# Residual rows read before the combination, and key tiles computed once instead of twice

## The chip, the cores and the metric

The kernel runs on one core of one Trainium2 chip. The metric is the device time of one execution, in microseconds. Everything is float32.

## What is computed

The reference is two models in a row on 512 tokens of width 1024.

The first has two layers over 528 positions (16 meta tokens in front). Each layer mixes attention with a recurrent branch and then runs a mixture of experts: a router picks one of 4 groups and 2 of its 8 experts for every token, each chosen expert computes `(silu(x w1) * (x w3)) w2`, and the layer ends in

```
y = gate0 * expert_row0 + gate1 * expert_row1          (per token)
h = layer_norm(ALPHA * h + y) * ln2_g + ln2_b
```

The second model is one block with three branches on 512 latent tokens and 256 context tokens. Branches a and b are attentions with 8 query heads and 2 key/value heads of 64: a sees a window, b everything. Keys are `h @ w_in[:, key columns]`, 128 columns for each branch (head 0 in the first 64, head 1 in the last). Those of b are normalised (`rms_norm`), and the latent keys of both are turned by a rotary embedding; context keys are not.

## The kernel before, in words

The program is a list of stages. Within a stage every engine has its own instruction list and they meet through semaphores; at a stage's end all engines meet, SyncE clears the stage's semaphores, and they meet again. So nothing of one stage's compute overlaps the next stage's. DMAs are issued by SyncE (SP queue), ScalarE (ACT queue) and GpSimd (indirect ones).

**The experts' stage** (`experts`) walks over blocks of 64 token slots. For each block SyncE loads the expert's weights w1, w3 (`load_up`) and w2 (`load_down`, line 1944), 1 MB each, into one of two ring buffers as they come free; GpSimd gathers the block's token rows from `h_rows` in DRAM; TensorE transposes them, multiplies by w1 and w3 (line 2002), transposes the hidden rows and multiplies by w2 (line 2021); ScalarE stores the result into `y_rows` in DRAM with two DMAs of 128 KB (line 2078). Four experts' weights were loaded ahead of the stage, into buffers of their own (`k.early`, on the right side of SBUF); the first of them, `k.early[0]`, is used by the stage's first block and not again. SyncE's last instruction in the stage is the last `load_down`, which waits for the block three before the end. ScalarE waits for its last stores to land before it leaves the stage.

**The combination** (`combine`), once per layer, follows. The 528 tokens are 6 tiles of 88 rows. SyncE reads the residual rows of each tile from `h_rows` (line 2155, six DMAs of 352 KB). GpSimd gathers the two expert rows of each token from `y_rows` (line 2161, two indirect DMAs of 352 KB a tile, 12 in all), tile 0 first. ScalarE scales the first row by its gate (`weigh`, line 2185) once both gathers of the tile have landed; VectorE adds the second (line 2222) and the residual (line 2227), which together with the mean (line 2230) is `add_rows`; ScalarE squares and takes the root; VectorE normalises (`norm`, lines 2234 and 2236), TensorE transposes (line 2174), and the two engines empty PSUM into `k.h` (`finish`, lines 2203 and 2242). VectorE's order is add 0, add 1, norm 0, add 2, norm 1, finish 0, add 3, norm 2, finish 1, and so on. `k.right`, which holds the early buffers, is closed before it.

**The projections of attention** (`scale_inputs`, then `attend`). `scale_inputs` norms the inputs of the second model and meanwhile loads the first weights: 2 MB for b's queries and the key columns. `attend` then computes tiles of 128 output columns, 8 contraction steps each, two matmul instructions a step in the records. The tiles in order: 4 of b's queries, 8 of keys, 4 of a's queries, 6 of values. A key tile is (branch, head g, context or latent): the 64 columns of head g stand twice in the loaded weights, so that the tile holds the same head's keys in partitions 0 to 63 and again in 64 to 127. Tiles of b are followed by a matmul that sums squares (line 2467) and a norm on VectorE, latent ones of both branches by a matmul that turns them (line 2477). TensorE runs through all this in a written order; ScalarE copies each tile out of PSUM (line 2486). SyncE reloads the weight ring for a's queries after tile 4 (line 2429) and for the values after the last key tile.

**The attention itself** (`branch_attention`) computes two query heads at a time (`score`, line 2620): head e = 0 from partitions 0 to 63, e = 1 from 64 to 127, both against the keys of the same head g. That is why the keys stand in both halves.

Of the kernel before, what the change touches and what calls it, by code (L numbers as in the profile page):

```python
# [16 lines left out]
P = 128  # L17
D = 1024
KD = D // P
SEQ, META = 512, 16  # L20
T = SEQ + META
TC = 88
NC1 = T // TC
# [33 lines left out]
CTX = 256  # L57
# [1048 lines left out]
def rwkv(k, a, li):  # L1106
    nc, ps = k.nc, k.ps
    r, key, v = (k.u[:, n * RT:(n + 1) * RT, :] for n in range(3))
    decay_in, rate_in, gate_in = (k.u[:, 3 * RT + n, :] for n in range(3))
    with ExitStack() as tmp:  # L1110
        kk = k.sb("kk", [P, RT, T], stack=tmp)
        sig = [k.sb(f"sig{d}", [P, RT, T], stack=tmp) for d in range(2)]
        rate = [k.sb(f"rate{d}", [P, RT, T], stack=tmp) for d in range(2)]
        y = k.sb("y", [P, RT, T], stack=tmp)
        rwkv_prep(k, a, li, key, v, decay_in, rate_in, gate_in, kk, sig, rate, y)
        wkv(k, a, r, key, v, kk, sig, rate, y)
        k.right = ExitStack()
        k.early = [early_place(k, n) for n in range(SOON)]
        k.early_in = [k.right.enter_context(nc.semaphore(f"early_in{n}")) for n in range(PRE)]
        mix_close(k, a, li, r, key, v, rate, sig, kk, y, gate_in)  # L1120
# [521 lines left out]

def expert_weights(a):
    return [a[n].rearrange("l e (p t) n -> (l e) p t n", p=P) for n in ("moe_w1", "moe_w3", "moe_w2")]


def moe(k, a, li):


    nc, ps = k.nc, k.ps  # L1650
    with ExitStack() as tmp:
        def sb(name, shape, dt=F32):
            return k.sb(name, shape, dt, stack=tmp)
        gate = sb("gate", [TC, 2, NC1])
        dest = sb("dest", [TC, 2, NC1], I32)
        slots = sb("slots", [SLOT, NBLK + 1], I32)
        owner = sb("owner", [1, DYN], I32)
        pairs = sb("pairs", [1, 1], I32)
        k.early += [early_place(k, n) for n in range(SOON, PRE)]
        with ExitStack() as rt:  # L1660
            route(k, a, li, rt, gate, dest, slots, owner, pairs)
        with ExitStack() as ex:
            experts(k, a, li, ex, slots, owner, pairs, k.early, k.early_in)
        k.right.close()
        with ExitStack() as cb:
            combine(k, cb, gate, dest)

# [211 lines left out]
def experts(k, a, li, ex, slots, owner, turns_left, early, early_in):  # L1879
# [34 lines left out]
    with k.stage("blank_set", "passed_gp", "passed_pe", "passed_act", *[f"{n}{z}" for n in names for z in Z],  # L1914
# [11 lines left out]
        def _(sp):  # L1926
# [32 lines left out]
            load_down(1, owner[0:1, bass.ds(n_turns * 2 + (AHEAD - 1), 1)], (z, c))  # L1959

# [170 lines left out]
def combine(k, cb, gate, dest):  # L2131
# [3 lines left out]
    hr = k.sb("c_h_rows", [TC, NC1, D], stack=cb)  # L2135
# [4 lines left out]
    with k.stage(*landed_names, *[f"h{j}_in" for j in range(NC1)], "first_weighted", "weighted", "summed", "meant",  # L2140
                 "squared", "rooted", "inverted", "normed", "c_turned", "act_kept", "dve_kept") as (block, *sems):
        landed, h_in = sems[0:NC1], sems[NC1:2 * NC1]
        (first, weighted, summed, meant, squared, rooted, inverted, normed, turned, act_kept,
         dve_kept) = sems[2 * NC1:]
# [6 lines left out]

        @block.sync
        def _(sp):
            for j in range(NC1):
                sp.dma_start(hr[:, j, :], k.h_rows[j * TC:(j + 1) * TC, :]).then_inc(h_in[j], 16)
# [62 lines left out]
        def _(dve):  # L2218
            def add_rows(j):
# [5 lines left out]
                dve.wait_ge(h_in[j], 16)  # L2225
                pt = row(j).rearrange("s (p t) -> s p t", t=KD)
                dve.scalar_tensor_tensor(pt, hr[:, j, :].rearrange("s (t p) -> s p t", t=KD), ALPHA, pt,
# [10 lines left out]
            def finish(j):  # L2238
# [5 lines left out]
                last.then_inc(dve_kept, 1)  # L2244
            add_rows(0)
# [39 lines left out]
def scale_inputs(k, a, t, x, mod, gain, hl, hc, w_in, ring, ring_in):  # L2285
# [8 lines left out]
    with k.stage("ctx_landed", "squared", "squared_ctx", "summed", "summed_ctx", "root", "root_ctx",  # L2294
# [5 lines left out]
        def _(sp):  # L2300
# [80 lines left out]
def attend(k, a, at, w_in, hl, hc, ys, cq, lf, cv, ring, ring_in):  # L2381
# [11 lines left out]
    tiles = ([("q", 1, m, 1) for m in range(4)] + [("k", n, g, c) for n in (1, 0) for g in range(2) for c in range(2)]  # L2393
# [7 lines left out]
    def home(i):  # L2401
        kind, n, m, lat = tiles[i]
        if kind == "q":
            return q[n][:, m, :]
        return v[:, m, :] if kind == "v" else (kt[n][:, m, CTX:W] if lat else kt[n][:, m, 0:CTX])
# [10 lines left out]
    with ExitStack() as t:  # L2416
# [5 lines left out]
        with k.stage("table_in", "qa_in", "v_in", "made", "emptied", "summed", "rooted", "normed", "turned", "roped",  # L2422
                     "ab_chain", also=ring_in) as (
                block, table_in, qa_in, v_in, made, emptied, summed, rooted, normed, turned, roped, steps):
# [10 lines left out]
            def _(pe):  # L2435
                for what, i in order:
                    kind, n, m, lat = tiles[i]
                    w = cols(i)
                    if what == "tile":
# [4 lines left out]
                        if i == 4:  # L2444
                            pe.wait_ge(k_in, 16 * 8)
# [6 lines left out]
                        for f in range(KD):  # L2452
                            if kind == "q":
                                l, r = ring[0][:, f, m * P:(m + 1) * P], hl[:, f, :]
                            elif kind == "k":
                                l, r = ring[1][:, f, (2 * n + m) * P:(2 * n + m + 1) * P], (hc, hl)[lat][:, f, :]
# [24 lines left out]
            def _(act):  # L2481
                for what, i in order:
                    w = cols(i)
                    if what == "tile":
# [7 lines left out]
                        last.then_inc(emptied, 1)  # L2492
                    elif what == "sum":
# [31 lines left out]
def branch_attention(k, a, at, w_in, hl, hc, q, kt, v, ys, cq, lf, cv):  # L2525
# [61 lines left out]
    with k.stage("tables_in", "wc_even", "wc_odd", "scored", "peaked", "weighed", "sunk", "normed", "turned",  # L2587
# [24 lines left out]
        def _(pe):  # L2612
            def score(i):
# [3 lines left out]
                for bank, off, cols, key in pieces(tiles):  # L2617
                    for e in range(2):
# [3 lines left out]
                                         rhs=kt[n][hd, g, key:key + cols], start=True, stop=True)  # L2622
# [1121 lines left out]
```

## Time and profile before

| | us |
|---|---|
| median of 3 runs | 3941.36 (3934.95 to 3941.69) |
| the profiled execution, its own time | 3947.0 |
| its span in the profile | 3945.2 |
| TensorE busy | 3355.2 |
| VectorE busy | 1496.2 |
| ScalarE busy | 811.6 |

Times in rows are microseconds from the start of the span. A timeline row gives the start, the time that the group of instructions covers, the engine, the line, what is written and read, how many instructions are merged, and in brackets how long the engine had been idle before and what ended that. An engine's name with a q behind it (SPq, ACTq) is the queue side of the engine: the instruction that issues a DMA, not the transfer. A window row gives, for each engine, the busy time, then the clock granted to TensorE (1.00 is full), the mean busy share of the 16 DMA engines and what they moved.

### The profile page before, as it was taken

Reading aid. Unit: us, or ns where it says so; the run is one execution under the profiler, and the core shown is the slowest. Engines: PE = TensorE matmul, PEld = TensorE weight load, DVE = VectorE, ACT = ScalarE, POOL = GpSimd, SP = SyncE. Lnnn points to the kernel's source line nnn. Section 1 sums busy time; section 2 is a strip of 40 time slices with the busy share of each in tenths; the row PEclk is TensorE's granted clock in tenths of the full one; section 3 lists DMA queues with packets and bytes.
Section 4 is the critical chain, followed back from the end, with each engine's and each line's share of the span. In section 5 each row is a group of like instructions: output and inputs, shape, how many; then the busy total and the mean of one; then the engine's idle time right before and its main releaser. Section 6 shows DMA issues by size and latency. Waiting matters only on the chain. (4 is left out here: it accounts for less than half of the span.)

```text
span 3945.2 us, 73875 instructions
## 1 busy us (share of the span) xinstructions
PE 3355.2 (85%) x31960; PEld 2250.6 (57%) x31960; DVE 1496.2 (38%) x2771; ACT 811.6 (21%) x1670; POOL 308.1 (8%) x499
## 2 busy tenths in 40 slices
PE   4898799986874897889958747999988899999998
PEld 0666599774443665789745423567656644444443
DVE  2244455532113444455441125355456521144411
ACT  3111322111112112222021123133343100010000
POOL 0000112001111000211001110000033000000000
PEclk7999799988996998899969977999999999999999
DMA  8210300227994010300148983110010122222221
GB/s 295 74 48 25 129 4 4 77 97 283 395 368 128 32 33 25 131 4 5 76 166 351 411 280 80 33 33 22 12 54 1 66 74 70 80 75 75 62 71 39
DMA packets 181484, 422.88 MB, mean 107 GB/s; under 512 B 33897, under 2 KB 128489, under 8 KB 152633
## 3 DMA queue, kind: packets, MB, share of 16 engines
q1 hardware_dynamic: 162201, 384.26, 26.5%
q0 software_dynamic: 8736, 17.32, 1.7%
q10 hardware_dynamic: 10240, 16.79, 1.3%
q8 instruction: 244, 4.00, 0.4%
q14 instruction: 63, 0.52, 0.0%
HBM read 401.60 MB, written 50.54 MB: 115 GB/s over the span
## 5 line engine op out<-in xcount | busy, mean ns | idle before, releaser
L3401 PE MATMUL ps<-h_lat,wt 128*128 128x512 f32 x704 | 304.7, 596 | 5.9 <-ACT h_lat L3458 5.9
L2002 PE MATMUL ps<-e_w,e_xt 128*64 128x256 f32 x1792 | 226.6, 409 | 64.0 <-DMA e_w<-in_moe_w 62.5
L709 PE MATMUL ps<-h,win 128*128 128x264 f32 x960 | 233.1, 397 | 16.9 <-DVE pad L858 15.3
L2002 PEld LDWEIGHTS ps<-e_w,e_xt 128*64 128x64 f32 x1792 | 149.9, 148 | 162.9 <-issue 78.9
L3401 PEld LDWEIGHTS ps<-h_lat,wt 128*128 128x128 f32 x704 | 134.6, 191 | 176.0 <-issue 174.4
L709 PEld LDWEIGHTS ps<-h,win 128*128 128x128 f32 x960 | 180.7, 193 | 67.4 <-issue 38.7
L2109 DVE TENSOR_TENSOR e_hid<-ps,e_silu 64x256 f32<-64x256 f32 x64 | 39.3, 614 | 399.5 <-ACT e_silu L2068 399.5
L3358 PE MATMUL ps<-h_lat,wt 128*128 128x512 f32 x384 | 169.5, 600 | 9.9 <-DMA wt<-in_w_in 9.9
L3419 PE MATMUL ps<-ff_up,wt 128*128 128x512 f32 x352 | 152.2, 592 | 0.0
L1315 PE MATMUL ps<-inv,nt 48*48 48x48 f32 x3520 | 130.5, 207 | 12.0 <-issue 10.8
L1414 DVE COPY_PREDICATED inv<-level,ps 112x384 f32<-112x384 int32 x176 | 103.5, 588 | 84.1 <-PE ps L1315 75.5
L3358 PEld LDWEIGHTS ps<-h_lat,wt 128*128 128x128 f32 x384 | 73.8, 193 | 103.1 <-issue 93.0
L2021 PE MATMUL ps<-e_w,e_hid_t 128*64 128x512 f32 x448 | 112.8, 622 | 18.5 <-DMA e_w<-in_moe_w 13.9
L1248 ACT ACTIVATE nt<-ps 112x192 f32<-112x192 f32 x220 | 72.6, 330 | 231.2 <-PE ps L1304 228.0
L1315 PEld LDWEIGHTS ps<-inv,nt 48*48 48x48 f32 x3520 | 109.4, 123 | 14.8 <-issue 13.4
L1304 PE MATMUL ps<-inv,by_bet 48*48 48x48 f32 x3520 | 104.9, 206 | 11.9 <-issue 5.9
L3419 PEld LDWEIGHTS ps<-ff_up,wt 128*128 128x128 f32 x352 | 66.9, 190 | 84.2 <-issue 83.7
L1312 PE MATMUL ps<-nt,inv 48*48 48x48 f32 x2816 | 104.2, 207 | 4.7 <-issue 3.7
L2174 PE MATMUL ps<-ident,c_y 88*128 88x88 f32 x96 | 17.2, 361 | 101.1 <-DVE c_y L2236 101.1
L1304 PEld LDWEIGHTS ps<-inv,by_bet 48*48 48x48 f32 x3520 | 93.7, 122 | 16.1 <-issue 9.6
L2072 ACT ACTIVATE e_hid_t<-ps 128x128 f32<-128x128 f32 x64 | 17.7, 277 | 401.5 <-PE ps L2010 401.5
L2663 PE MATMUL ps<-wc,h_lat 128*128 128x256 f32 x384 | 91.5, 383 | 5.8 <-DVE log_f L2774 4.7
(564 smaller groups left out, 6386.6 us busy)
## 6 DMA issues: line engine op xcount, KB each, us to landing
e_w<-in_moe_w SPq DMA_DIRECT2D x168, 1024.0 KB
wmod<-in_w_mod SPq DMA_DIRECT2D x24, 1024.0 KB, 14.2
early<-in_moe_w SPq DMA_DIRECT2D x24, 1024.0 KB, 14.8
wt<-in_w_up SPq DMA_DIRECT2D x22, 1024.0 KB, 5.1
y_rows<-e_y ACTq DMA_DIRECT2D x128, 128.0 KB
win<-in_w_in SPq DMA_DIRECT2D x10, 1536.0 KB, 6.6
wt<-in_w_in SPq DMA_DIRECT2D x12, 1024.0 KB, 7.7
wt<-in_w_down SPq DMA_DIRECT2D x16, 704.0 KB, 4.8
```

What stands on the lines that cost most here:

```text
L709: last = pe.matmul(ps[:, 7, 0:HT], lhsT=ring[(s + 1) % 2][:, i, o:o + P], rhs=k.h[:, i, h * HT:(h + 1) * HT], start=(i == 0), stop=(i == K ...
L1248: act.activation(nt[z][:, :, :], ps[0:R, bank_a(c), 0:RT * WC].rearrange("p (f n) -> p f n", f=RT), ACT.Copy).then_inc(x_kept[z], 1)
L1304: last = pe.matmul(ps[hw, a0, f * WC:(f + 1) * WC], lhsT=by_bet[z][hw, f, 0, :], rhs=inv[z][hw, 0, f, :], start=True, stop=True)
L1312: pe.matmul(ps[hw, a0, f * WC:(f + 1) * WC], lhsT=inv[z][hw, 1, f, :], rhs=nt[z][hw, f, :], start=True, stop=True)
L1315: last = pe.matmul(ps[hw, a0, (RT + f) * WC:(RT + f + 1) * WC], lhsT=nt[z][hw, f, :], rhs=inv[z][hw, 1, f, :], start=True, stop=True)
L1414: dve.copy_predicated(inv[z][0:R, :, :, :], k.level[0:R, level, d:d + 2, None, :].to_broadcast([R, 2, RT, WC]), ps[0:R, a0, 0:2 * RT * WC] ...
L2002: last = pe.matmul(ps[half, 2 + z, 0:EH], lhsT=xt[z][:, f, :], rhs=w[:, f, :], start=(f == 0), stop=(f == KD - 1))
L2021: last = pe.matmul(ps[half, 4 + z, :], lhsT=hid_t[z][:, t, :], rhs=m2[:, t, q * 512:(q + 1) * 512], start=(t == 0), stop=(t == 1))
L2663: last = pe.matmul(ps[:, 7, 0:cols], lhsT=lhsT, rhs=rhs, start=(i == 0), stop=(i == KD - 1))
L3358: last = pe.matmul(o, lhsT=w[:, i, m % 2 * P:(m % 2 + 1) * P], rhs=hl[:, i, :], start=(i == 0), stop=(i == KD - 1))
L3401: last = pe.matmul(o, lhsT=w[:, i, m % 2 * P:(m % 2 + 1) * P], rhs=hl[:, i, :], start=(i == 0), stop=(i == KD - 1))
L3419: last = pe.matmul(o, lhsT=w[:, i, :], rhs=up[:, f, :], start=(f == 0), stop=(f == FT - 1))
```

## The change

Residual rows. After its last `load_down`, still in the experts' stage, SyncE issues three DMAs that read all 528 residual rows into the three tensors of `k.early[0]`, two tiles of 88 rows each; it first waits for the block that used those buffers. The combination no longer issues the six DMAs of line 2155; VectorE waits once, for all three reads, before its first `add_rows`. `k.right` is closed after the combination.

Keys. The key columns are loaded once (two DMAs of 512 KB in place of eight of 256 KB). A key tile is (branch, context or latent), 4 in place of 8, with head 0 in partitions 0 to 63 and head 1 in 64 to 127. During the value tiles ScalarE copies each half to the other half's partitions, into a second tile (8 copies of 64 partitions), and `score` takes the tile in which head g stands in the half e.

```diff
+def residual_rows(k):
+    return [t[0:TC, :, :].rearrange("s a b -> s (a b)").rearrange("s (j n) -> s j n", j=2) for t in k.early[0]]
...
         with ExitStack() as ex:
             experts(k, a, li, ex, slots, owner, pairs, k.early, k.early_in)
-        k.right.close()
         with ExitStack() as cb:
             combine(k, cb, gate, dest)
+        k.right.close()
...
             load_down(1, owner[0:1, bass.ds(n_turns * 2 + (AHEAD - 1), 1)], (z, c))
+            z, c = spot(first.index(("early", 0)))
+            sp.wait_ge(down[z], c + 1)
+            for n, dst in enumerate(residual_rows(k)):
+                sp.dma_start(dst, k.h_rows[2 * n * TC:(2 * n + 2) * TC, :].rearrange("(j s) n -> s j n", j=2)
+                             ).then_inc(k.h_back, 16)
...
-        @block.sync
-        def _(sp):
-            for j in range(NC1):
-                sp.dma_start(hr[:, j, :], k.h_rows[j * TC:(j + 1) * TC, :]).then_inc(h_in[j], 16)
...
-                dve.wait_ge(h_in[j], 16)
...
+            dve.wait_ge(k.h_back, 48)
             add_rows(0)
...
-                for g in range(2):
-                    for c in range(2):
-                        at = (4 * n + 2 * g + c) * 64
-                        sp.dma_start(ring[1][:, :, at:at + 64], w_in[:, :, c0 + g * 64:c0 + (g + 1) * 64]
-                                     ).then_inc(ring_in[2], 16)
+                sp.dma_start(ring[1][:, :, n * P:(n + 1) * P], w_in[:, :, c0:c0 + P]).then_inc(ring_in[2], 16)
...
-    tiles = ([("q", 1, m, 1) for m in range(4)] + [("k", n, g, c) for n in (1, 0) for g in range(2) for c in range(2)]
+    tiles = ([("q", 1, m, 1) for m in range(4)] + [("k", n, 0, c) for n in (1, 0) for c in range(2)]
...
+                def swap(i):
+                    n, lat = tiles[i][1], tiles[i][3]
+                    if lat:
+                        act.wait_ge(roped, turned_tiles.index(i) + 1)
+                    elif i in normed_tiles:
+                        act.wait_ge(normed, normed_tiles.index(i) + 1)
+                    else:
+                        act.wait_ge(emptied, i + 1)
+                    for g in range(2):
+                        act.activation(kt[n][(1 - g) * HD:(2 - g) * HD, 1, keys_of(i)],
+                                       kt[n][g * HD:(g + 1) * HD, 0, keys_of(i)], ACT.Copy).then_inc(swapped, 1)
...
                         last.then_inc(emptied, 1)
+                        if V < i <= V + 4:
+                            swap(i - V + 3)
...
-                                         rhs=kt[n][hd, g, key:key + cols], start=True, stop=True)
+                                         rhs=kt[n][hd, (e + g) % 2, key:key + cols], start=True, stop=True)
```

## Rows read from the trace of the kernel before

**Rows 1.** the page: busy time of the engines (us, share of span, instructions)
```profile
PE 3355.2 (85%) x31960; PEld 2250.6 (57%) x31960; DVE 1496.2 (38%) x2771; ACT 811.6 (21%) x1670; POOL 308.1 (8%) x499
```
**Rows 2.** timeline, layer 1, experts' end into the combination (start, us, engine, line)
```profile
1168.21 3.67 PE L2002 MATMUL ps<-e_w,e_xt 128*64 128x256 f32 x32
...
1168.28 0.33 SPq L1944 DMA_DIRECT2D e_w<-in_moe_w  x1
...
1175.56 3.79 ACTq L2078 DMA_DIRECT2D y_rows<-e_y  x4
...
1184.08 2.50 SPq L2155 DMA_DIRECT2D c_h_rows<-h_rows  x6
1184.91 0.98 POOL L2161 DMA_INDIRECT c_y<-y_rows,dest  x1 [27.21 <-POOLq L151]
1186.20 0.98 POOL L2161 DMA_INDIRECT c_y<-y_rows,dest  x1 [0.31 <-issue]
...
1201.20 1.15 ACT L2185 ACTIVATE c_y<-c_y,gate 88x1024 f32<-88x1024 f32 x1 [26.07 <-DMA c_y<-y_rows,dest]
1202.38 1.28 DVE L2222 SCALAR_TENSOR_TENSOR c_y<-c_y,gate 88x1024 f32<-88x1024 f32 x1 [24.34 <-ACT c_y L2185]
...
1205.63 0.15 DVE L2230 TENSOR_SCALAR c_st<-c_st 88x1 f32<-88x1 f32 x1
...
1215.92 1.19 DVE L2242 TENSOR_SCALAR h<-ps,par 128x88 f32<-128x88 f32 x4
...
1217.02 1.27 DVE L2222 SCALAR_TENSOR_TENSOR c_y<-c_y,gate 88x1024 f32<-88x1024 f32 x1
...
1222.36 1.27 DVE L2222 SCALAR_TENSOR_TENSOR c_y<-c_y,gate 88x1024 f32<-88x1024 f32 x1
```
**Rows 3.** timeline, layer 2, the same places
```profile
2332.04 0.98 POOL L2161 DMA_INDIRECT c_y<-y_rows,dest  x1 [26.59 <-POOLq L151]
...
2348.87 1.15 ACT L2185 ACTIVATE c_y<-c_y,gate 88x1024 f32<-88x1024 f32 x1 [26.56 <-DMA c_y<-y_rows,dest]
2350.05 1.28 DVE L2222 SCALAR_TENSOR_TENSOR c_y<-c_y,gate 88x1024 f32<-88x1024 f32 x1 [24.84 <-ACT c_y L2185]
...
2365.83 1.28 DVE L2222 SCALAR_TENSOR_TENSOR c_y<-c_y,gate 88x1024 f32<-88x1024 f32 x1
```
**Rows 4.** busy time by window (engines, PEclk, DMA share, GB/s), experts' end
```profile
1172.00:1175.00 3.00, 2.74 (x20) 1.17 (x18) 0.93 (x2) 1.39 (x4) 0.00 (x0) 1.00 0.53 164
...
1178.00:1181.00 3.00, 0.00 (x0) 0.00 (x0) 0.04 (x1) 0.00 (x0) 0.00 (x0) 0.90 0.38 88
```
**Rows 5.** DMA queues, 1184 to 1188 us (packets, MB, share of 16 engines)
```profile
q1 hardware_dynamic: 185, 0.70, 51.3%
...
q0 software_dynamic: 45, 0.00, 0.5%
```
**Rows 6.** DMA queues, 1203 to 1209 us: the gathers alone
```profile
q0 software_dynamic: 530, 1.30, 101.8%
```
**Rows 7.** the combination's tile c_y: time from issue to landing
```profile
DMA to landing us min/median/max: 11.0/18.4/22.0
```
**Rows 8.** timeline of TensorE in the projection stage of attention
```profile
2476.63 0.59 PE L2467 MATMUL ps<-ab_sq,ones_h 128*128 128x256 f32 x2
2477.06 1.02 PE L2477 MATMUL ps<-k_b,rot 128*128 128x512 f32 x2
...
2494.27 13.90 PE L2460 MATMUL ps<-h_lat,wab 128*128 128x512 f32 x32
```
**Rows 9.** DMA issues, 2440 to 2500 us: line 2429's load, KB, us to landing
```profile
wab<-in_w_in SPq DMA_DIRECT2D x1, 2048.0 KB, 8.1
```
**Rows 10.** timeline, value tiles of that stage
```profile
2546.91 0.38 ACT L2486 ACTIVATE v_ab<-ps 128x256 f32<-128x256 f32 x1 [3.07 <-PE ps L2460]
```
**Rows 11.** the tile e_silu: a copy to other partitions
```profile
L2068 ACT ACTIVATE e_silu<-ps x64: 375/375/377, 931.1 to 2320.4; 64x256 f32<-64x256 f32 x64
```
**Rows 12.** window of the score matmuls alone (line 2620)
```profile
2555.00:2890.00 335.00, 47.79 (x368) 28.85 (x368) 0.97 0.13 42
```

More of the change, by code:

```diff
@@ L1118, in rwkv @@
         k.early = [early_place(k, n) for n in range(SOON)]
+        k.h_back = k.right.enter_context(nc.semaphore("h_back"))
         k.early_in = [k.right.enter_context(nc.semaphore(f"early_in{n}")) for n in range(PRE)]
@@ L2134, in combine @@
     y = k.sb("c_y", [TC, NC1, 2, D], stack=cb)
-    hr = k.sb("c_h_rows", [TC, NC1, D], stack=cb)
+    hr = residual_rows(k)
     sq = k.sb("c_sq", [TC, 2, D], stack=cb)
@@ L2139, in combine @@
     landed_names = [f"y{j}_in" for j in range(NC1)]
[L2140 to L2144, printed above, removed]
+    with k.stage(*landed_names, "first_weighted", "weighted", "summed", "meant", "squared", "rooted", "inverted",
+                 "normed", "c_turned", "act_kept", "dve_kept", also=[k.h_back]) as (block, *sems):
+        landed = sems[0:NC1]
+        first, weighted, summed, meant, squared, rooted, inverted, normed, turned, act_kept, dve_kept = sems[NC1:]
         def row(j):
@@ L2224, in add_rows @@
                 dve.wait_ge(weighted, j + 1)
-                dve.wait_ge(h_in[j], 16)
                 pt = row(j).rearrange("s (p t) -> s p t", t=KD)
-                dve.scalar_tensor_tensor(pt, hr[:, j, :].rearrange("s (t p) -> s p t", t=KD), ALPHA, pt,
+                dve.scalar_tensor_tensor(pt, hr[j // 2][:, j % 2, :].rearrange("s (t p) -> s p t", t=KD), ALPHA, pt,
                                          ALU.mult, ALU.add, accum_out=stat(0, j)).then_inc(summed, 1)
@@ L2404, in home, with keys_of @@
             return q[n][:, m, :]
-        return v[:, m, :] if kind == "v" else (kt[n][:, m, CTX:W] if lat else kt[n][:, m, 0:CTX])
+        return v[:, m, :] if kind == "v" else kt[n][:, 0, keys_of(i)]
+    def keys_of(i):
+        return slice(CTX, W) if tiles[i][3] else slice(0, CTX)
     normed_tiles = [i for i, x in enumerate(tiles) if x[0] != "v" and x[1] == 1]
@@ L2422, in attend @@
         with k.stage("table_in", "qa_in", "v_in", "made", "emptied", "summed", "rooted", "normed", "turned", "roped",
-                     "ab_chain", also=ring_in) as (
-                block, table_in, qa_in, v_in, made, emptied, summed, rooted, normed, turned, roped, steps):
+                     "swapped", "ab_chain", also=ring_in) as (
+                block, table_in, qa_in, v_in, made, emptied, summed, rooted, normed, turned, roped, swapped, steps):
             @block.sync
@@ L2444, in _ @@
                         if i == 4:
-                            pe.wait_ge(k_in, 16 * 8)
+                            pe.wait_ge(k_in, 16 * 2)
                         if i == QA:
@@ L2455, in _ @@
                             elif kind == "k":
-                                l, r = ring[1][:, f, (2 * n + m) * P:(2 * n + m + 1) * P], (hc, hl)[lat][:, f, :]
+                                l, r = ring[1][:, f, n * P:(n + 1) * P], (hc, hl)[lat][:, f, :]
                             else:
```

## The prediction

> **What bounds the kernel now.** I read the page first: TensorE is busy for 85% of the span, no other engine for more than 38% [rows 1]. That is an average. Since the engines meet at each stage's end, a change is worth what it takes off its own stage, so I went to the timeline of the stages that the diff touches.
>
> In the projection stage TensorE is the bound. Its matmul records follow each other without a gap: 32 of 512 columns in 13.90 us [rows 8], while ScalarE sat idle for 3.07 us before a copy of 0.38 us [rows 10].
>
> In the combination TensorE does nearly nothing. The six reads of residual rows are issued at 1184.08, the first gather at 1184.91, and ScalarE, which starts the work of tile 0, stands idle until 1201.20, released by a gather's DMA [rows 2]. Until 1188 us the DMA engines moved 0.70 MB of residual rows and next to nothing of the gathers [rows 5]: the reads were there first and hold the engines. Later, with the gathers alone, those engines are full as well (share 101.8%) and move 1.30 MB in 6 us, 217 GB/s [rows 6]. So the first 16 us of a combination are DMA time, a third of whose load is residual rows: 6 x 352 KB = 2.16 MB beside 4.33 MB of gathers. Behind it, VectorE is the bound: its add of one tile starts 5.34 us after the one before (1217.02, 1222.36) with no idle time noted [rows 2].
>
> **Part 1, the combination's start.** Without the residual reads, tile 0 needs its two gathers only. The second is issued at 1187.18, 2.27 us after the first issue began (1186.20 + 0.98 - 1184.91) [rows 2]. The bytes of a gather begin more than 2.1 us after its issue: the first one's ended at 1185.89, and by 1188 its queue had moved 0.00 MB [rows 5]; I take 2.4. The 0.72 MB of two gathers at 217 GB/s are 3.3 us [rows 6]. Sum: 2.3 + 2.4 + 3.3 = 8.0 us from the first issue to the landing of tile 0. Today it is 1201.20 - 1184.91 = 16.3 us in layer 1 [rows 2] and 2348.87 - 2332.04 = 16.8 us in layer 2 [rows 3]. Gain: 8.3 + 8.8 = 17.1 us. The ends: without the 2.4 us of delay tile 0 lands at 5.6, a gain of 21.9 for both layers; the slowest I allow is a landing as fast as the quickest gather beside the residual reads, 11.0 us [rows 7], for the second one too, so 12.3, and a gain of 8.5.
>
> The Trainium skill (DMA: Bandwidth & Descriptors, section Anatomy of one DMA) gives a DMA issued by GpSimd about 2.0 us plus its bytes at 436 GB/s. By that page, as an estimate, tile 0 would land at 2.3 + 2.0 + 0.8 = 5.1 us and the gain be 22.9. The trace agrees with its fixed part (over 2.1 us) and not with its rate: half of it is what rows show of these gathers.
>
> **Part 2, the pace behind tile 0.** Today VectorE waits for gathers between tiles 0 and 3: add 3 starts 14.64 us after add 0 in layer 1 (1202.38 to 1217.02) [rows 2] and 15.78 us after it in layer 2 (2350.05 to 2365.83) [rows 3]. Between them lie three adds, two norms and one finish. Two steady steps are two of each, 10.7 us; one more add is 3.40 us (1202.38 to 1205.78) and the finish that is not in it 1.19 us [rows 2]: 10.7 + 3.4 - 1.2 = 12.9. A tile's two gathers take 3.3 us of DMA against 5.34 of VectorE, so the gathers stay ahead once tile 0 is there. I allow 0.3 a layer for ScalarE, whose root of tile 0 comes later in the row than in steady state, and take 13.2: gain 1.4 + 2.6 = 4.0 us. Ends: 0 (the gathers keep today's spacing) and 4.6.
>
> **Part 3, where the residual reads go.** SyncE's last weight load is issued at 1168.28 [rows 2]. The three reads follow it in the same queue, all weights ahead of them, so TensorE waits for none of it; the wait on the first block's `down` was fulfilled long ago, and behind SyncE's reads nothing of its own is queued. The DMA engines are 0.53 busy from 1172 to 1175 and 0.38 from 1178 to 1181 [rows 4], with stores. Today 0.70 MB of them had come by 1188 [rows 5]; if their bytes began a microsecond after the issue at 1184.08 (an estimate), that is 0.70 MB in 2.9 us, about 245 GB/s, and at that rate 2.16 MB are 8.8 us of otherwise free engines. From 1172 that is 1181 alone and about 1184 beside the stores. So they land about when the combination begins (1184.08), and tile 0's add, not before 1193, does not wait. What they cost is the last stores: four are issued from 1175.56 to 1179.35 [rows 2], and ScalarE waits for them before the stage ends. Bounds a layer: nothing if the stores slip between, and 6 us if the stores came behind all the reads that are left at 1178 (8.8 less the free half of the time since 1172). In a fair alternation the last pair, 0.38 of 3 us or 1.1 us of engine time [rows 4], takes about double: I take 1.5, so -3.0 us for both layers.
>
> The same page (section Queues, rings and completion order) says that each DMA engine turns between its queues packet by packet; by it the fair share is the right case, and the price would be the 1.1 to 1.5 us used; no run here shows it yet.
>
> **Part 4, the key tiles.** TensorE loses four tiles: two latent (16 records of 512 columns: 13.73 / 2 = 6.87 us, since the 13.90 of [rows 8] hold 0.17 of tail) and two context ones (16 records of 256; two take 2477.06 - 2476.63 = 0.43 us, so 3.44) [rows 8]: 20.6 us. With them go two sums of squares, 0.86 and 0.43, and two turns of 0.86 (two records of 512). Sum 20.6 + 1.3 + 1.7 = 23.6 us. All of it is on the path, as TensorE has no gap there. What could be late next: the weights of a's queries, 8.1 us after their issue [rows 9]. They are issued as the key tiles begin and needed after them; the key tiles still last 20.6 + 4.7 = 25 us (49 today). The value weights are issued when the keys are done and have four query tiles, over 27 us, of cover. The loads of the key columns shrink from 2 MB to 1 MB, in a stage where nothing waits for them: nothing.
>
> The 8 copies are ScalarE's. A copy of 64 partitions by 256 columns into other partitions takes 0.375 us [rows 11]; for 512 columns I take 0.6. Behind a value tile stand at most two of 0.6, with the tile's own 0.38: 1.6 us where 3.07 + 0.38 are free [rows 10]. Two value tiles follow the third pair and one the last. Cost 0, hidden by the value tiles' matmuls; without that cover 8 copies would be 4 us. Bounds for the part: 22 to 25 us.
>
> **Sum.** 17.1 + 4.0 - 3.0 + 23.6 = 41.7 us off 3947.0, the profiled execution's time, gives 3905.3. The median of the runs shown is 5.6 below that execution, so the forecast is 3900. All ends together: gain 21.9 + 4.6 + 0 + 25 = 51.5, or 8.5 + 0 - 12 + 22 = 18.5; times 3890 and 3923.
>
> **Rivals.** (a) The combination gives nearly nothing: the gathers are the DMA load that matters (4.33 of 6.5 MB) and the moved reads hold back the stage before. For it: gathers alone fill the engines [rows 6]. Against: tile 0 waits for two of twelve gathers only. Price: 8.5 - 8, nearly 0, and part 4 alone: 3941.4 - 23.6 = 3918. Chance 0.16.
>
> (b) The key part gives nothing, because ScalarE or VectorE becomes the bound of the key tiles, or a's query weights are late. For it: VectorE norms and turns each tile. Against: the idle times named above. Price: only 18 of 41.7 us: 3923. Chance 0.05.
>
> (c) Slower. The score matmuls go in pairs, one on each half of the partitions, and both halves read the same columns today; after the change they read two different tiles. Were the pairs side by side only for that reason, each would cost double: 47.8 us of matmuls and up to 28.9 of weight loads more [rows 12], 3900 + 77 = 3977 at most. It decides from 50 us, at which the gain is eaten and 0.2% lost. Against it: line 2002 writes two halves from two different moving tensors, w1 and w3, and does 32 records of 256 columns in 3.67 us, 0.115 each [rows 2], where records of 256 columns cost 0.215 each on the whole array [rows 8]. So different moving data do not stop pairs there. Chance 0.03.
>
> (d) The early reads or the copies do not do what they say (VectorE waits for the reads as long as before): within 2 us of (a). In its chance.
>
> **How the numbers follow.** Forecast 0.76, around 3900, own range 3891 to 3910. The rest: (a) 0.16, (b) 0.05, (c) 0.03. The range of 8 in 10 takes in the forecast's ends and most of (a): 3889 to 3917. This kernel's measurement tells no change from one of under 0.2% (8 us). Faster by more: the forecast, (a) and nearly all of (b), 0.95; same 0.02; slower 0.03.
>
> **What would show it.** In the profile after: the first ScalarE instruction of the combination about 8 us after the first gather's issue, not 16; add 3 about 13 us after add 0; the gap from the last store's issue to the first gather (today 1179.35 to 1184.91, 5.6 us) 1 to 2 us longer; SyncE's three issues right behind its last weight load; 4 key tiles, 23.6 us less of the projection stage, no idle TensorE in it, and the score matmuls' busy time at 47.8. A first tile that lands later than 11 us, or an experts' stage longer by 3 us or more, would make the forecast wrong by (a); a longer score window by (c).

## The result and the profile after

| | us |
|---|---|
| before, median of 4 runs | 3941.53 (3934.95 to 3945.72) |
| after, median of 4 runs | 3905.34 (3904.77 to 3905.90) |
| ratio | 0.9899, 95% interval 0.9885 to 0.9913 |
| span in the profile, before and after | 3945.2, 3903.1 |

By the medians the change makes the kernel 36 us faster (0.9%), by the ratio with its interval 40 us (34 to 45). The forecast was 3900, its range 3889 to 3917.

The timeline of the changed kernel, layer 1, from the experts' end into the combination (start, us, engine, line); it answers to [rows 2]:

```profile
1164.08 1.29 SPq L1969 DMA_DIRECT2D early<-h_rows  x3
...
1165.21 3.67 PE L2013 MATMUL ps<-e_w,e_xt 128*64 128x256 f32 x32 [1.70 <-DMA e_w<-in_moe_w]
...
1172.38 1.94 PE L2032 MATMUL ps<-e_w,e_hid_t 128*64 128x512 f32 x8 [0.57 <-DMA e_w<-in_moe_w]
...
1172.56 6.66 ACTq L2089 DMA_DIRECT2D y_rows<-e_y  x4
...
1177.21 0.69 DVE L2129 COPY e_y<-ps 128x512 f32<-128x512 f32 x1 [4.84 <-DMA y_rows<-e_y]
1185.68 0.98 POOL L2166 DMA_INDIRECT c_y<-y_rows,dest  x1 [29.60 <-SPq L149]
...
1194.24 1.15 ACT L2190 ACTIVATE c_y<-c_y,gate 88x1024 f32<-88x1024 f32 x1 [22.11 <-DMA c_y<-y_rows,dest]
...
1195.49 1.28 DVE L2227 SCALAR_TENSOR_TENSOR c_y<-c_y,gate 88x1024 f32<-88x1024 f32 x1 [17.59 <-ACT c_y L2190]
...
1209.51 1.27 DVE L2227 SCALAR_TENSOR_TENSOR c_y<-c_y,gate 88x1024 f32<-88x1024 f32 x1
```

Tile 0 starts 8.56 us after the first gather's issue (1194.24 - 1185.68), where it was 16.29. But the first gather is issued 20.47 us after TensorE's last expert block began (1165.21), where it was 16.70 [rows 2]. VectorE stood idle for 4.84 us before its last copy and was released by a store. In the kernel before it was 1.97 us, and the matmul released it:

```profile
1175.28 1.94 PE L2021 MATMUL ps<-e_w,e_hid_t 128*64 128x512 f32 x8 [0.46 <-ACT e_hid_t L2072]
...
1177.35 0.69 DVE L2118 COPY e_y<-ps 128x512 f32<-128x512 f32 x1 [1.97 <-PE ps L2021]
```

The same places in layer 2, to be read beside [rows 3]:

```profile
2306.20 3.67 PE L2013 MATMUL ps<-e_w,e_xt 128*64 128x256 f32 x32 [1.74 <-DMA e_w<-in_moe_w]
...
2319.01 0.69 DVE L2129 COPY e_y<-ps 128x512 f32<-128x512 f32 x1 [5.65 <-DMA y_rows<-e_y]
2327.69 0.98 POOL L2166 DMA_INDIRECT c_y<-y_rows,dest  x1 [31.59 <-SPq L149]
...
2335.18 1.15 ACT L2190 ACTIVATE c_y<-c_y,gate 88x1024 f32<-88x1024 f32 x1 [22.06 <-DMA c_y<-y_rows,dest]
...
2336.44 1.28 DVE L2227 SCALAR_TENSOR_TENSOR c_y<-c_y,gate 88x1024 f32<-88x1024 f32 x1 [16.74 <-ACT c_y L2190]
...
2349.82 1.27 DVE L2227 SCALAR_TENSOR_TENSOR c_y<-c_y,gate 88x1024 f32<-88x1024 f32 x1
```

Here tile 0 comes 7.49 us after the gather (16.83 before), and the gather 21.49 us after the last block; in the kernel before that was 2315.39 to 2332.04, 16.65 us.

TensorE in the projection stage, then ScalarE in it, which answer to [rows 8] and [rows 10], and third the window row of the score matmuls alone (line 2637; PE busy, PEld busy, clock, DMA share, GB/s), which answers to [rows 12]:

```profile
2436.10 3.62 PE L2464 MATMUL ps<-h_ctx,wab 128*128 128x256 f32 x16
...
2461.63 7.03 PE L2464 MATMUL ps<-h_lat,wab 128*128 128x512 f32 x16
...
2516.05 1.13 PE L2637 MATMUL ps<-k_a,q_a 64*128 64x256 f32 x8 [1.77 <-PEq L151]
```

```profile
2500.91 0.86 ACT L2495 ACTIVATE k_b<-k_b 64x256 f32<-64x256 f32 x2
2503.95 0.38 ACT L2501 ACTIVATE v_ab<-ps 128x256 f32<-128x256 f32 x1 [2.19 <-PE ps L2464]
2504.36 1.28 ACT L2495 ACTIVATE k_b<-k_b 64x512 f32<-64x512 f32 x2
2507.40 0.38 ACT L2501 ACTIVATE v_ab<-ps 128x256 f32<-128x256 f32 x1 [1.76 <-PE ps L2464]
```

```profile
2500.00:2890.00 390.00, 47.79 (x368) 28.84 (x368) 0.98 0.11 36
```

The key tiles begin at 2436.10, a's first query tile at 2461.63: 25.5 us, where 49 were spent. The two copies of a pair take 0.86 us (256 columns) and 1.28 us (512), and ScalarE still sits idle for 1.76 to 2.19 us before the copy of the value tile behind each pair. TensorE's records of the stage show no idle time. From the stage's first matmul to the first score matmul it is 2401.50 to 2516.05, 114.6 us; before, 2417.43 to 2555.49, 138.1. The score matmuls' busy time is 47.79 us, to the hundredth what it was [rows 12].

### The profile page after: what moved, and what is told of

It reads as the page before. It is cut to its first block and busy times, and to the rows that moved or that the text cites. A ratio compares the mean times of both kernels' runs of the same rounds, so it can differ in the third digit from the quotient of the medians.

```text
span 3903.1 us, 73678 instructions
## 1 busy us (share of the span) xinstructions
PE 3331.0 (85%) x31888; PEld 2236.9 (57%) x31888; DVE 1485.6 (38%) x2761; ACT 812.1 (21%) x1670; POOL 314.4 (8%) x499
## 5 line engine op out<-in xcount | busy, mean ns | idle before, releaser
L709 PE MATMUL ps<-h,win 128*128 128x264 f32 x960 | 233.4, 397 | 16.8 <-DVE pad L858 15.2
L1316 PE MATMUL ps<-inv,nt 48*48 48x48 f32 x3520 | 130.9, 207 | 10.6 <-issue 9.2
L1313 PEld LDWEIGHTS ps<-nt,inv 48*48 48x48 f32 x2816 | 88.4, 123 | 9.8 <-issue 8.1
```

The costliest lines, as they stand in the source:

```text
L709: last = pe.matmul(ps[:, 7, 0:HT], lhsT=ring[(s + 1) % 2][:, i, o:o + P], rhs=k.h[:, i, h * HT:(h + 1) * HT], start=(i == 0), stop=(i == K ...
L1313: pe.matmul(ps[hw, a0, f * WC:(f + 1) * WC], lhsT=inv[z][hw, 1, f, :], rhs=nt[z][hw, f, :], start=True, stop=True)
L1316: last = pe.matmul(ps[hw, a0, (RT + f) * WC:(RT + f + 1) * WC], lhsT=nt[z][hw, f, :], rhs=inv[z][hw, 1, f, :], start=True, stop=True)
```

## The experiments

All times are beside runs of the kernel before on the same chip. To read the traces I use one distance that drifts of other stages do not enter, the "whole distance": from TensorE's last w2 block of the experts (1175.28 before, layer 1) to VectorE's last gated add in the combination (add 5, 1227.71). "End" is the part from that block to the first gather, "landing" from there to ScalarE's first instruction on tile 0. The expectations count from the w1 block before it instead, which in the kernel before begins 7.1 us earlier. Each kernel has one trace, so differences under about a microsecond (the changed kernel's two traces differ by 0.6 and 0.7) say little.

| kernel | median | ratio (95%) | end, layers 1, 2 | landing | whole distance |
|---|---|---|---|---|---|
| before | | | 9.6, 9.6 | 16.3, 16.8 | 52.4, 54.1 |
| after | 3905.3 | 0.9899 (0.9885 to 0.9913) | 13.3, 14.0 | 8.6, 7.5 | 47.8, 46.8 |
| after, again | 3911.8 | 0.9922 (0.9906 to 0.9938) | 14.2, 15.1 | 8.4, 7.1 | 48.4, 47.5 |
| keys_only | 3923.3 | 0.9942 (0.9923 to 0.9960) | 9.6, 9.6 | 17.8, 16.8 | 55.2, 53.3 |
| reads_only | 3934.0 | 0.9965 (0.9953 to 0.9977) | 14.7, 15.6 | 8.2, 7.4 | 48.0, 48.2 |
| no_reads | 3897.3 | 0.9873 (0.9851 to 0.9895) | 9.6, 9.6 | 8.7, 7.8 | 43.4, 42.5 |
| late_kept | 3908.6 | 0.9892 (0.9872 to 0.9913) | 15.9, 15.3 | 8.9, 8.1 | 49.8, 48.6 |
| late_out | 3928.5 | 0.9941 (0.9926 to 0.9956) | 11.0, 11.0 | 18.8, 16.9 | 54.9, 53.1 |
| spread | 3923.6 | 0.9922 (0.9907 to 0.9938) | 15.4, 15.5 | 8.5, 7.0 | 49.4, 48.4 |
| late_out_spread | 3924.3 | 0.9926 (0.9910 to 0.9942) | 12.0, 12.1 | 13.4, 13.6 | 51.6, 50.7 |
| early_reads | 3929.5 | 0.9945 (0.9929 to 0.9961) | 9.5, 9.5 | 8.5, 6.8 | 43.4, 42.2 |
| own_buffer | 3906.2 | 0.9914 (0.9901 to 0.9928) | 16.0, 15.0 | 7.6, 7.3 | 48.7, 47.5 |
| gated | 3905.2 | 0.9912 (0.9894 to 0.9929) | 10.6, 10.9 | 7.9, 7.1 | 48.2, 48.5 |
| gated_own_buffer | 3906.1 | 0.9909 (0.9895 to 0.9922) | 9.5, 9.5 | 8.1, 8.4 | 47.8, 47.6 |

Three sets were timed on three chips: keys_only, reads_only, no_reads and late_kept (the kernel before 3945.4), then late_out, spread, late_out_spread and early_reads (3954.5), then the changed kernel again with own_buffer, gated and gated_own_buffer (3941.0). So ratios are compared, not medians, and a time named in an expectation of the first two sets has to be read 4 and 13 us higher. The ratios are estimates of their own; the quotients of the medians differ from them by up to 0.0015. The changed kernel gave 0.9899 and 0.9922, which is how far two sets of runs of one kernel lie apart here.

**Each part alone.** keys_only is the kernel before with the edits of `scale_inputs`, `attend` and `score`; reads_only has the others.

> The key part alone; the residual rows are read as before. Theory (the parts add, and the key part is TensorE's matmuls and nothing else): 23.5 us off the kernel before, 3918, with the combination as it was (tile 0 starts 16 us after the first gather's issue). Rival (part of what the changed kernel gained came from the fewer small DMAs of the key columns or from ScalarE): a gain clear of 23.5, under 20 or over 28.

> The residual rows' part alone; keys as before. Theory (combinations shorter by 8.4 and 11.7 us, experts' ends longer by 3.8 and 4.8): 11 to 13 us off, 3929 to 3931. Rival (the forecast's price of 3 us for the moved reads was right and the profile's longer ends are chance): 18 us off, 3923.

0.9942 is 23 us (16 to 30), 0.9965 is 14 us (9 to 18). The two sum to 37 us; the change as a whole gives 36 by its medians, 40 and 31 by its two ratios. The intervals do not tell 23.5 from 20 by themselves; the traces do: from the projection stage's first matmul to the first score matmul it is 114.3 us in keys_only and 138.1 in reads_only. For the reads, 18 lies at the interval's edge, so the time alone does not decide. The trace of reads_only has the longer ends again (14.7 and 15.6), and its whole distances are 10.3 us shorter in all than those of the kernel before, which speaks for 11 to 13.

**What the moved reads cost.** no_reads leaves out the three reads and the wait for them.

```diff
-            for n, dst in enumerate(residual_rows(k)):
-                sp.dma_start(dst, k.h_rows[...]).then_inc(k.h_back, 16)
...
-            dve.wait_ge(k.h_back, 48)
```

> The changed kernel with the residual reads left out altogether, and VectorE's wait for them (the residual added is then whatever lies in the buffer, so the output is not the reference's). Theory (the moved reads cost 8.6 us through the stores that share the DMA engines): 3896 to 3898, the distance from TensorE's last block of experts to the first gather back at 16.7 us in both layers, and VectorE's last copy there not waiting for a store. Rival (the ends are longer for another reason, such as the later close of the buffers or the barrier): no less than 3903, distance still over 20 us.

0.9873 against 0.9899 is 10 us, and against the second set's 0.9922 it is 19; the traces below give 8.7. The end is back at 9.6 us in both layers, and the copy waits for the matmul only:

```profile
1173.07 1.94 PE L2027 MATMUL ps<-e_w,e_hid_t 128*64 128x512 f32 x8 [0.46 <-ACT e_hid_t L2078]
1173.36 3.79 ACTq L2084 DMA_DIRECT2D y_rows<-e_y  x4
...
1175.14 0.69 DVE L2124 COPY e_y<-ps 128x512 f32<-128x512 f32 x1 [1.97 <-PE ps L2027]
1182.70 0.98 POOL L2161 DMA_INDIRECT c_y<-y_rows,dest  x1 [27.21 <-SPq L149]
```

So the reads cost 4.3 to 4.4 us a layer of the whole distance (47.8 - 43.4, 46.8 - 42.5), 8.7 in all. Left where they were before the change they cost 9.0 and 11.6 a layer (52.4 - 43.4, 54.1 - 42.5). So 11.9 of 20.6 us are gone, a little over half of their price. In the changed kernel their packets last from about 1169 to 1181 us. The DMA queues in those twelve microseconds (packets, MB, share of 16 engines; q1 carries the reads, q10 the stores):

```profile
q1 hardware_dynamic: 544, 2.10, 51.2%
q10 hardware_dynamic: 472, 0.77, 22.6%
```

The reads' 2.10 MB take the whole of it, with all but the last 0.01 MB of the stores among them. Without the reads the stores' last packets had moved by 1181 in the kernel before, and the first gather was issued at 1184.91.

**Reads later.** late_kept and late_out hold the reads back:

```diff
             sp.wait_ge(down[z], c + 1)
+            z, c = in_loop(n_turns, -1)
+            sp.wait_ge(y_kept[z], c + 1)            # late_kept
+            sp.wait_ge(y_out[z], c * 32 + 32)       # late_out, in its place
```

> The changed kernel, but SyncE holds the three residual reads until VectorE has copied the last block's rows out (wait on the last y_kept), so that they run under the last store, the stages' meeting and the first gathers' start-up. Theory: the wait of VectorE's last copy for a store goes (2.8 and 3.2 us), of the last store's own delay about 1 us a layer stays; the reads, 8.8 us, end some 9 to 10 us after that copy, before tile 0's add needs them (17 us after it): 3898 to 3900. Rival A (the reads then run into the gathers and what is won is given back there): 3904 to 3908, tile 0 later than 10 us after the first gather's issue. Rival B (the longer end has nothing to do with the order): 3905.

The copy no longer waited for a store, and yet the end grew to 15.9 us and the ratio is that of the changed kernel: the theory missed, and rival A missed as well (tile 0 came 8.9 us after the first gather, not later than 10). The time is as rival B has it, but the order does matter: it took away the copy's wait and the stores waited elsewhere. The DMA queues of late_kept (packets, MB, share of 16 engines), 1182 to 1185 us and then 1185 to 1188:

```profile
q1 hardware_dynamic: 117, 0.47, 72.6%
q10 hardware_dynamic: 3, 0.01, 1.0%
```

```profile
q1 hardware_dynamic: 120, 0.45, 52.1%
q10 hardware_dynamic: 107, 0.17, 18.6%
```

ScalarE had issued its last store by 1180.40 and SyncE its reads from 1179.12. For three microseconds the stores' queue moved 3 packets, then 107. By 1185 the reads had moved 0.23 MB (1179 to 1182) and 0.47, together 0.70, about one read of the three (0.72). So the last stores stood behind roughly the first read and alternated with the rest, which lasted until about 1195. That it was just this read is my reading of the sums. From 1182 to 1184.5 the stores' queue moved no packet at all, while the reads held 0.73 of the engines' time and a quarter of it was free.

> The changed kernel, but SyncE issues the three residual reads only when the experts' last store has landed. Where the wait stood on y_kept, the last store's packets moved some 6 us late, behind the reads, and the meeting of the engines came 4 us after them while the reads still ran. Theory (stores issued after reads wait behind them, and the stage's end waits for the stores only): the distance from TensorE's last block to the first gather is 16.7 us as without reads; the reads run from about 1181 to 1192, under the meeting and the first two gathers; tile 0 starts 8 to 11 us after the first gather; 3898 to 3901. Rival (the stage's end waits for SyncE's own reads to land): that distance is 16.7 + 9 to 11 us, 26 or more, and the time 3912 or more.

The theory held for the end, but for 1.4 us, and failed for the sum. The end is 11.0 us with the reads in flight, so the stage's end does not wait for SyncE's reads; the 1.4 us over 9.6 I put down to SyncE, which now issues last before the engines meet; no run shows that apart. But tile 0 landed 18.8 us after the first gather. The queues from 1187 to 1192 us show why, with the gathers' issue begun at 1187.16:

```profile
q1 hardware_dynamic: 198, 0.76, 70.9%
q0 software_dynamic: 75, 0.12, 12.4%
```

The reads hold 0.71 of the engines and the gathers 0.12. The reads met the gathers, as in the kernel before.

**Reads on more engines.** In the row above, and in late_kept's (0.73), the reads run nearly alone and their queue takes 0.71 to 0.73 of 16 engines. That is about 11 of 16 (0.69).

```diff
-                sp.dma_start(dst, src).then_inc(k.h_back, 16)
+                for lo, hi in ((0, 80), (80, TC)):
+                    sp.dma_start(dst[lo:hi], src[lo:hi]).then_inc(k.h_back, 16)
```

> The changed kernel with each of the three residual reads cut in two by partitions, 80 rows and 8 rows, at the same place. The reads of 88 rows kept the DMA engines busy to 0.71 to 0.73 where they ran nearly alone, as if 11 of 16 worked. Theory (rows are dealt out over a number of engines that divides 88, and 80 gives all 16): the reads are through in about 6.5 us instead of 9.5, and the two blocks' stores behind them are held up less: distance from the last block to the first gather 18 to 19.5 us instead of 20.5 to 21.5, 3900 to 3903. Rival (the share is the memory's limit on these rows): no change, 3905, and six issues instead of three.

> Both: reads after the last store has landed, cut into 80 and 8 rows. Theory: the reads are over when the gathers' bytes begin; distance to the first gather 16.7 us, tile 0 some 8 us after it: 3897 to 3899, as without any reads. Rival (reads spread over all engines then share them with the first gathers): tile 0 later than with the reads on 11 engines, 3900 or more.

The queue of the reads from 1174 to 1176 us, in spread and then in the changed kernel:

```profile
q1 hardware_dynamic: 129, 0.45, 104.8%
```

```profile
q1 hardware_dynamic: 125, 0.49, 70.5%
```

The second row is of 1172 to 1174, where the changed kernel's stores move next to nothing (0.03 MB). And the copy of spread, from its timeline:

```profile
1182.42 0.69 DVE L2130 COPY e_y<-ps 128x512 f32<-128x512 f32 x1 [7.74 <-DMA y_rows<-e_y]
```

With 80 rows a read takes all 16 engines (share 104.8%), so the cause of the 0.7 was named rightly. But it moves 0.45 MB in two microseconds, where 11 engines moved 0.49: the five engines more brought no rate. The gain did not follow: from 1172 to 1178 the reads moved 1.37 MB, close to two of the three, and the stores' queue not one packet, though its next two stores were issued at 1172.14 and 1172.78. The copy waited 7.74 us instead of 4.84, and the end went to 15.4 us. The second set of the changed kernel has copies that waited 7.19 and 7.13 us and ends of 14.2 and 15.1, so that the cut made things worse is not shown; that it did not help is. With the reads behind the last store the cut did help (0.43 to 0.56 MB in two microseconds, where late_out had 0.30 to 0.38), landing 13.4 instead of 18.8, and the whole distance still was 3 to 4 us over that of the changed kernel.

**Reads early.** early_reads puts SyncE's three reads between the weight loads at the start of the experts' loop.

> The changed kernel with the three reads moved to the start of the experts' loop on SyncE's queue, between weight loads. Theory (that stretch is bound by the DMA engines, TensorE waiting for weights): the reads' own time goes on the path, 5 to 10 us a layer, and the end of the stage is free of them (16.7 us): 3897 + 10 to 20 = 3907 to 3917. Rival (there is room between the weight loads): 3897 to 3900, the best place for them.

The end and the combination were as without reads (43.4, 42.2). From the experts' first memset to their last block, the stage took 274.8 and 272.1 us (910.08 to 1184.92, 2060.68 to 2332.75), where the changed kernel took 261.5 and 258.4: 13 to 14 us a layer for 2.16 MB, more than the 5 to 10 expected. (The other kernels took 255 to 262 us here, so each difference is good to some 3 us.) There TensorE waits for weights, and the reads' time is on the path. 0.9945 is no better than leaving the reads where they were (keys_only, 0.9942).

**The store's buffer, and two reads in the combination.** own_buffer gives the last block's rows a buffer of their own (`y_last`), so the copy waits for no store. gated leaves one read at the experts' end; the others wait in the combination:

```diff
+        @block.sync
+        def _(sp):
+            for n, gate_on, done in ((1, 0, h1_in), (2, 2, h2_in)):
+                sp.wait_ge(landed[gate_on], 32)
+                sp.dma_start(hr[n], k.h_rows[...]).then_inc(done, 16)
```

> The changed kernel itself, as the mark for the three others on the same chip. From TensorE's last block to VectorE's fourth add (add 3) it took 44.3 and 43.6 us, and 39.8 and 38.9 without the reads. Both theories: the same again within 2 us, ratio to the kernel before 0.990.

To add 3 it took 43.9 us in layer 2, as expected, but 47.0 in layer 1, 2.7 more. The excess lies ahead of the last w2 block:

```profile
1170.71 3.36 PE L2032 MATMUL ps<-e_w,e_hid_t 128*64 128x512 f32 x8 [2.73 <-DMA e_w<-in_moe_w]
```

TensorE waited 2.73 us for the last weights. Their load stands just ahead of the reads in SyncE's queue. It was issued at 1161.45, 9.26 us before this block, where the kernel before had its weights without a wait after 7.00 (1168.28 to 1175.28). The block then ran at a granted clock of 0.57 (1170 to 1174) and took 3.36 us instead of 1.94. Seven of the kernels issue a read right behind that load: in 6 of their 14 layers the block waited 0.57 to 2.73 us for the weights, in the changed kernel's first trace 0.57 and 0.92. In the 14 layers of the seven others it never did; there ScalarE released it after 0.46. So the reads can delay the last weights too, and the whole distance, which begins with that block, leaves this out: mostly some tenths of a microsecond, 2.3 us here.

> The changed kernel with a buffer of its own for the last block's rows, so that VectorE's last copy does not wait for a store two blocks back. Theory 1 (that wait, 2.8 to 3.2 us, is most of the 3.8 and 4.8 us that the moved reads cost): distance from the last block to the first gather 17.5 to 19 us, 2 to 3 us a layer less than the changed kernel. Theory 2 (the last stores have to queue behind the reads' packets in any case; the waiting buffer only shows it earlier): the copy is early, but the distance stays at 20 us or more, and the time is that of the changed kernel.

The timeline of own_buffer, and its queues from 1178 to 1181 and from 1181 to 1184 us:

```profile
1173.53 0.69 DVE L2143 COPY e_y_last<-ps 128x512 f32<-128x512 f32 x1 [1.88 <-PE ps L2033]
1174.41 1.13 ACTq L2090 DMA_DIRECT2D y_rows<-e_y_last  x2
1187.51 0.99 POOL L2170 DMA_INDIRECT c_y<-y_rows,dest  x1 [33.22 <-SPq L149]
```

```profile
q1 hardware_dynamic: 135, 0.53, 50.8%
q10 hardware_dynamic: 135, 0.22, 21.2%
```

```profile
q1 hardware_dynamic: 46, 0.14, 15.2%
q10 hardware_dynamic: 75, 0.11, 11.4%
```

The copy came 2 us after the block, the last store was issued by 1175.54, and the stores' queue still moved 0.22 MB from 1178 to 1181 and 0.11 MB after 1181. The ends are 16.0 and 15.0 us, 23.0 and 22.1 as the expectation counts. Theory 2 holds: the wait at the buffer only shows the queue behind the reads, and taking it away saves nothing.

> The changed kernel with only the first of the three reads (tiles 0 and 1) at the experts' end; the second is issued in the combination when tile 0's gathers have landed, the third when tile 2's have. Theory (behind tile 0 the DMA engines have room beside VectorE's 5.3 us a tile): distance to the first gather 17 to 18.5 us, tile 0 about 8 us after it, add 3 at most 1.5 us later behind add 0 than in the changed kernel, the last add as early; 40.5 to 42.5 us from the last block to add 3, 2 us a layer less in the time. Rival (the gathers fill the engines until the last tile, so each read behind them delays a tile): add 0 to add 5 longer by 3 us or more, no gain.

> Both of the two edits. Theory 1 with the room behind tile 0: nearly the time without any reads, 40 to 41.5 us from the last block to add 3, 6 us in all below the changed kernel. Theory 2: as gated alone.

The end is 10.6 us, and 9.5 with both edits, tile 0 as early as hoped. Then, in gated:

```profile
1192.76 8.25 SPq L2166 DMA_DIRECT2D early<-h_rows  x2
...
1194.02 1.28 DVE L2234 SCALAR_TENSOR_TENSOR c_y<-c_y,gate 88x1024 f32<-88x1024 f32 x1 [15.95 <-ACT c_y L2197]
...
1207.77 1.92 DVE L2240 SCALAR_TENSOR_TENSOR c_y<-early,c_y 88x1024 f32<-88x1024 f32 x1 [4.57 <-DMA early<-h_rows]
...
1211.82 1.27 DVE L2234 SCALAR_TENSOR_TENSOR c_y<-c_y,gate 88x1024 f32<-88x1024 f32 x1
```

The read of tiles 2 and 3, issued at 1192.76, kept VectorE waiting 4.57 us; add 3 came 17.8 us after add 0 instead of 14.0, and add 5 28.5 and 29.2 us after it instead of 24.7 and 24.1. The rival was right, and theory 1 of gated_own_buffer missed with it. The whole distance, 47.6 to 48.5 us, is that of the changed kernel, and so are the ratios, 0.9909 to 0.9914 within 0.9885 to 0.9938.

To keep the residual rows in SBUF from the routing on would need no read. By my count of the tensors' sizes their 24 KB a partition do not fit beside the experts' buffers; this was not tried.

## Why the prediction came out as it did

| step | forecast, us | measured, us |
|---|---|---|
| part 1, tile 0 earlier | 17.1 | 7.7 + 9.3 = 17.1 |
| part 2, pace behind it | 4.0 | 0.6 + 2.4 = 3.0 |
| part 3, price of the moved reads | -3.0 | -(3.8 + 4.8) = -8.6 |
| part 4, key tiles | 23.6 | 23.5 |
| sum | 41.7 | 35.0 |

The measured column is from the traces of before and after: 16.29 - 8.56 and 16.83 - 7.49; add 0 to add 3, 14.64 - 14.02 and 15.78 - 13.38; 20.47 - 16.70 and 21.49 - 16.65; 138.1 - 114.6. The runs give 36.2.

Parts 1, 2 and 4 name the right waits and work; part 3 names the right cost, the last stores, at about a third of its size.

Part 4 came out to 0.1 us, and for the reason given: four key tiles fewer and no idle TensorE. Its cover held: two copies of 512 columns took 1.28 us against the 1.2 assumed and hid behind the value tiles. Rival (c) is refuted: different tiles in the two halves cost the score matmuls nothing. So is (b), by the 23.5.

That part 1 agrees to a tenth is luck twice over. Tile 0 came 0.6 us later than the 8.0 forecast in layer 1 and 0.5 earlier in layer 2, and the terms of the 8.0 are not what happened. In layer 1 the gathers' queue had moved 0.07 MB by 1188, so their bytes began less than 2.4 us after the issue at 1185.68, and 0.71 MB by 1191, as much as tile 0 has: 5.3 us after the issue. ScalarE started only at 1194.24. The forecast had no term for these last 3 us and made up for them by adding up the issues and the 2.4 us, which overlap. Whether bytes of later gathers went ahead of tile 0's last ones or the landing is reported late, no run here tells. So the 2.4 us ahead of the bytes, in which the forecast saw the fixed part of about 2.0 us that the Trainium skill (DMA: Bandwidth & Descriptors, section Anatomy of one DMA) gives, are not borne out by this trace. Part 2's 13.2 us is what no_reads shows in both layers; in the changed kernel it was 14.0 and 13.4.

Rival (a) had a real point and a wrong price. Its sign, an experts' stage longer by 3 us or more, did show (3.8 and 4.8), but the whole distances became 11.9 us shorter in all, so the combination gave clearly more than nothing. The sign was set too low to tell the two apart. The range, said to take in most of (a), also ends at 3917, below (a)'s own 3918.

The mis-sized step is part 3's sentence "In a fair alternation the last pair ... takes about double: I take 1.5". It has four errors. The reads were taken as 8.8 us of engines from one short window [rows 5]; they took 12 in the changed kernel and 14 in late_kept (1181 to 1195), so they meet more of the stores. It priced the last pair only; the changed kernel's trace shows the store two blocks back held up too, and VectorE's copy with it. The alternation does not begin at once: in late_kept the stores' queue moved 3 packets in 3 us beside 117 of the reads. And once it begins it is even in packets, not in bytes: in own_buffer, from 1174 to 1182, the reads moved 333 packets and the stores 370, but 1.29 MB against 0.61, and the last stores, issued by 1175.54, moved until after 1182. Beside that sentence, part 3's "so TensorE waits for none of it" held in only 8 of the 14 layers in which a read followed the last weights directly.

The rule that I set beside it (the Trainium skill, DMA: Bandwidth & Descriptors, section Queues, rings and completion order) does not by itself give the 1.5 us. It says that an engine drains a whole packet of one queue, typically some 9 to 17 descriptors, before it turns to the next. The packets counted in the rows above hold 3.9 KB on average on the reads' queue and 1.6 KB on the stores', and nothing shows that they are the packets of that section. If each row of 4 KB is one descriptor, a read of 176 rows on 11 engines puts 16 on each, which could be one such packet (an estimate from that section's figure). This fits the whole read that went first in late_kept, and not the even exchange after it. Nor does turn-taking at the engines explain why the stores stood still while a quarter of the engines' time was free. That speaks for a wait ahead of the engines, perhaps where descriptors are made; no run here shows it apart.

The upper bound of 6 us a layer covered it, which is why 3905 lay inside the range; the forecast's gain was 41.4 us from the median, the measured one 36.2. I had also called the window behind the weights "otherwise free engines". No window was free. What the reads add to the whole distance, over no_reads (43.4 and 42.5), is 4.3 to 4.4 us a layer in the changed kernel (5.0 in its second set), 4.4 to 5.7 in reads_only, own_buffer and gated_own_buffer, 4.8 to 6.0 in gated, 5.9 to 6.0 in spread, 6.1 to 6.4 in late_kept, 8.2 behind the last store with the cut, 9.0 to 11.8 where all three reads or more meet the gathers at once (before, keys_only, late_out), and 13 to 14 among the weights, there by the length of the experts' stage. The reads take 12 to 14 us, and no gap on the path is as long.

## What to carry to other kernels

A transfer moved off the front of a stage is paid again where it lands: before counting it as hidden, find the stores issued beside it whose landing somebody waits for, and charge them with more than a fair share: in late_kept about one whole read of 704 KB went first, in spread 1.37 MB. Look also at the transfer that stands ahead of it in the same queue: here the last weights came up to 2.3 us late. A transfer needs a gap as long as itself; here I estimate the gap at some 6 us (in the kernel before, the last store was in by 1181 and the first gather's bytes came after 1187) for 12 to 14 us of reads, and every placement tried paid the difference somewhere. Work that is computed twice only to change its place in the partitions is worth removing where the engine that computes it is the bound and another one has idle time of known length.

## What the runs showed of the hardware that I had not expected

Reads of 88 rows use 0.69 to 0.74 of the 16 DMA engines when alone, with 80 rows all of them (1.01 to 1.07). The Trainium skill (DMA: Bandwidth & Descriptors, section Why a DMA increments its semaphore by 16 and not by 1) says that a DMA runs on the largest number up to 16 that divides the outer size of both its sides, which is 11 for 88 and 16 for 80; the trace agrees (11 of 16 is 0.69). The rate does not follow the number: 11 engines moved 0.30 to 0.50 MB in two microseconds and 16 moved 0.43 to 0.56. What made late_out's and late_kept's reads (some 160 GB/s) slower than the changed kernel's (up to 245) on the same eleven is open.

A copy on ScalarE from one half of the partitions to the other, SBUF to SBUF, took 0.41 to 0.43 us for 64 x 256 and 0.63 for 64 x 512 (the pairs of 0.86 and 1.28 above, halved), where a copy of 128 partitions from PSUM in place takes 0.38 and 0.60. The forecast had taken 0.375 and 0.6.
